# Gates and branch projections with tokens in rows in a hybrid attention / SSD / expert layer

## What is computed

```python
g_na, g_ssd = jnp.split(jax.nn.sigmoid(gates), 2, axis=-1)
mixed = (g_na * (na @ lp['w_na_proj']) + g_ssd * (ssd @ lp['w_ssd_proj'])) @ lp['w_out']
x = x + g1 * mixed
```

## Time and profile before

| | |
|---|---|
| Median of 3 runs | 3015.32 us (3013.15 to 3019.16) |
| Span of the profiled execution | 3014.4 us |
| TensorE busy, in matmuls | 2316.1 us, 77% |
| VectorE busy | 2148.8 us, 71% |
| ScalarE busy | 1338.9 us, 44% |
| GpSimd busy | 1199.5 us, 40% |
| Moved by DMA | 868.48 MB, mean 288 GB/s |

### The profile page before, as it was taken

One profiled execution on the slowest core, in us unless ns is written; L12 is line 12 of the kernel. 1 busy time (PEld: TensorE's weight loads), 2 busy tenths in 40 slices (PEclk: granted clock), 3 DMA queues, 4 the chain that ended last, 5 costly groups with the idle time before them and its releaser, 6 DMA issues.

```text
span 3014.4 us, 39129 instructions
## 1 busy us (share of the span) xinstructions
PE 2316.1 (77%) x15054; PEld 2048.9 (68%) x15054; DVE 2148.8 (71%) x2801; ACT 1338.9 (44%) x2319; POOL 1199.5 (40%) x793
## 2 busy tenths in 40 slices
PE   6799999999999999999999950000233339999997
PEld 2578889988888898999997950000232328888886
DVE  1344445877778853444454699999999988999987
ACT  1233334566777773433334420000698934434443
POOL 0000000134334310000000676666788856767763
PEclk8799999999999999999999985555555559999998
DMA  9887776545454559876554369999999968999996
GB/s 392 329 304 295 291 291 232 184 156 173 172 180 154 173 197 371 319 260 240 191 192 167 140 263 422 392 364 363 403 421 422 422 259 308 372 365 376 361 375 235
DMA packets 152796, 868.48 MB, mean 288 GB/s; under 512 B 18865, under 2 KB 31169, under 8 KB 74705
## 3 DMA queue, kind: packets, MB, share of 16 engines
q1 hardware_dynamic: 68578, 449.03, 40.3%
q0 software_dynamic: 73872, 406.08, 34.8%
q10 hardware_dynamic: 10160, 10.88, 1.0%
HBM read 836.81 MB, written 27.39 MB: 287 GB/s over the span
## 4 chain that ended last, share of the span: by engine, by line
PE 50%; DVE 22%; DMA 9%; POOL 8%; issue 8%; ACT 3%; DVEq 0%; ACTq 0%; SPq 0%; POOLq 0%
PE bank L1805 28%; DVE u_ring L1664 9%; POOL u_ring L730 8%; PE bank L1791 8%; PE bank L2205 7%; DMA raw<-in_tiles 3%; DMA v_got<-in_v_rest,expert 3%; PE bank L1830 2%; DVE w_lo L1210 2%; DVE peer_g L1705 2%; DMA u_ring<-in_peer_u,expert 1%; DVE conv L1324 1%; DMA v_raw<-in_v_dense 1%; PE bank L2180 1%; DVE decay_s L1361 1%
## 5 line engine op out<-in xcount | busy, mean ns | idle before, releaser
L1210 DVE TENSOR_TENSOR w_lo<-raw,w_hi 128x1024 fp32r<-128x1024 f32 x450 | 581.6, 1304 | 564.6 <-ACT w_hi L775 558.6
L775 ACT ACTIVATE w_hi<-raw 128x1024 fp32r<-128x1024 f32 x482 | 500.6, 1057 | 561.1 <-PE bank L1805 327.3
L1805 PE MATMUL bank<-h_lo,w_hi 128*128 128x256 f32 x2048 | 593.7, 290 | 24.7 <-DVE w_lo L1210 16.0
L1805 PE MATMUL bank<-h_hi,w_lo 128*128 128x256 f32 x2048 | 582.8, 285 | 0.0
L1805 PE MATMUL bank<-h_hi,w_hi 128*128 128x256 f32 x2048 | 582.6, 284 | 0.0
L730 POOL DMA_INDIRECT u_ring<-in_peer_u,expert x256 | 508.3, 1985 | 166.7 <-DVE act_p L1664 85.1
L1805 PEld LDWEIGHTS bank<-h_lo,w_hi 128*128 128x128 f32 x2048 | 395.3, 193 | 69.5 <-issue 37.0
L1664 DVE CUSTOM_DVE_ANT_0 u_ring<-u_ring,h_t 128x2048 f32<-128x2048 f32 x192 | 430.7, 2289 | 9.3 <-DMA u_ring<-in_peer_u,expert 7.8
L737 POOL DMA_INDIRECT v_got<-in_v_rest,expert x256 | 358.5, 1401 | 180.1 <-DVE peer_g L1705 137.1
L1805 PEld LDWEIGHTS bank<-h_hi,w_lo 128*128 128x128 f32 x2048 | 395.5, 193 | 0.7
L1805 PEld LDWEIGHTS bank<-h_hi,w_hi 128*128 128x128 f32 x2048 | 395.3, 193 | 0.0
(11 more groups left out here) (317 smaller groups left out, 4760.8 us busy)
## 6 DMA issues: line engine op xcount, KB each, us to landing
raw<-in_tiles SPq DMA_DIRECT2D x337, 1024.0 KB, 5.6
v_raw<-in_v_dense SPq DMA_DIRECT2D x128, 660.0 KB, 7.2
s_t<-in_states POOLq DMA_DIRECT2D x8, 512.0 KB, 7.3
y_hi_rows<-y_hi_e POOLq DMA_DIRECT2D x16, 256.0 KB, 2.4
y_lo_rows<-y_lo_e POOLq DMA_DIRECT2D x16, 256.0 KB, 6.3
gate_rows<-gate_buf ACTq DMA_DIRECT2D x8, 512.0 KB, 6.7
y_hi<-y_hi_rows POOLq DMA_DIRECT2D x8, 512.0 KB, 8.3
y_lo<-y_lo_rows POOLq DMA_DIRECT2D x8, 512.0 KB, 4.2
```

What stands on the lines that cost most here:

```text
L775: act.activation(w_hi[:, i % RING], raw[:, slot % SLOTS, (n % 2) * 2 * CH:(n % 2 + 1) * 2 * CH], ACT.Copy) \
L1210: dve.tensor_tensor(w_lo[:, i % RING], raw[:, n // 2 % SLOTS, (n % 2) * 2 * CH:(n % 2 + 1) * 2 * CH], w_hi[:, i % RING].bitcast(F32), ALU. ...
L1805: ins = pe.matmul(spot if x.shape[1] == KT else spot.rearrange("p (s t) -> p s t", s=NS), w[:, col], moving, start=start and k == 0 and m ...
```

## The change

`gates`, `nap` and `ssd` are made by `tokens_out` in place of `features_out`, so their banks hold tokens in partitions; the gate rows, the products and the sum (`mix_t`, formerly `mix_f`) take that form too, with the same sizes. `tokens_out` gets the arguments that the two depths of `ssd` need. The sum is turned by TensorE: `turn_mix(p)` is eight transposes of 128x128 into banks 4 and 5 or 6 and 7, in the order behind half 1 of `ssd` 2, 4 and 6 and of `out` 0. `mixed_hi` and `mixed_lo` then split it from those banks, behind half 3 of the same. Two pairs of semaphores become one each (`kv_saved` for `k_saved` and `v_saved`, `res_in` for `x2_in` and `g1_in`).

The diff, cut (left out: new shapes in declarations, the renamed semaphores' other uses):

```diff
...
         y_lo = at("y_lo", [P, NS, 2 * KT, P], F32R, 152)
-        gate_n = at("gate_n", [P, 2, 4, T], F32, 48)
-        gate_y = at("gate_y", [P, 2, 4, T], F32, 104)
-        gated = at("gated", [P, 4, T], F32, 184)
-        mix_f = at("mix_f", [P, KT, T], F32, 64)
+        gate_n = at("gate_n", [P, 2, NS, CH], F32, 48)
+        gate_y = at("gate_y", [P, 2, NS, CH], F32, 104)
+        gated = at("gated", [P, NS, CH], F32, 184)
+        mix_t = at("mix_t", [P, 4, NS, CH], F32, 64)
...
         mix_sum = sem("mix_sum")
+        mix_turn = sem("mix_turn")
...
         mix_ready = sem("mix_ready")
-        x2_in = sem("x2_in")
-        g1_in = sem("g1_in")
+        res_in = sem("res_in")
...
-            pool.wait_ge(v_saved, 16)
+            pool.wait_ge(kv_saved, 16 * 5)
...
             for s, name in enumerate(("x_prompt", "x_sample")):
-                pool.dma_start(x2_t[:, s, :], a[name][0]).then_inc(x2_in, 16)
+                pool.dma_start(x2_t[:, s, :], a[name][0]).then_inc(res_in, 16)
...
                 pool.wait_ge(row_saved[n], 64 * len([i for i in saved_rows if i % 2 == n]))
-            pool.dma_start(g_rows[0:8, :], mod_rows[:, 2 * D:3 * D]).then_inc(g1_in, 16)
-            pool.dma_start(g_rows[8:9, :], a["ada_b"][:, 2 * D:3 * D]).then_inc(g1_in, 16)
+            pool.dma_start(g_rows[0:8, :], mod_rows[:, 2 * D:3 * D]).then_inc(res_in, 16)
+            pool.dma_start(g_rows[8:9, :], a["ada_b"][:, 2 * D:3 * D]).then_inc(res_in, 16)
...
                                       row[32 * t:32 * t + NS, i % 2, :]).then_inc(row_saved[i % 2], 16)
+
+            def mixed_hi(p):
+                act.wait_ge(mix_turn, p + 1)
+                for n_ in range(2):
+                    ins = act.activation(mix_hi[:, 4 * p + 2 * n_:4 * p + 2 * n_ + 2, :],
+                                         psum[4 + 2 * (p % 2) + n_][:].rearrange("p (b t) -> p b t", b=2), ACT.Copy)
+                ins.then_inc(mix_split, 1)
...
                     act.wait_ge(evac_a, ACT_DUE[ACC_OF["gates", j]])
-                    act.dma_start(gate_rows[j].rearrange("p b t -> p (b t)"),
+                    act.dma_start(gate_rows[j].rearrange("p s n -> p (s n)"),
                                   gate_buf[:, j % 2].rearrange("p s n -> p (s n)")).then_inc(gate_saved[j % 2], 16)
-                elif kind == "ssd" and j % 2 and h == 7:
-                    p = j // 2
-                    act.wait_ge(mix_sum, p + 1)
-                    act.activation(mix_hi[:, 4 * p:4 * p + 4], mix_f[:, 4 * p:4 * p + 4], ACT.Copy).then_inc(mix_split, 1)
+                elif kind == "ssd" and j and j % 2 == 0 and h == 3:
+                    mixed_hi(j // 2 - 1)
                 elif kind == "out":
+                    if j == 0 and h == 3:
+                        mixed_hi(3)
...
+            def mixed_lo(p):
+                dve.wait_ge(mix_split, p + 1)
+                for n_ in range(2):
+                    b = 4 * p + 2 * n_
+                    ins = dve.tensor_tensor(mix_lo[:, b:b + 2, :],
+                                            psum[4 + 2 * (p % 2) + n_][:].rearrange("p (b t) -> p b t", b=2),
+                                            mix_hi[:, b:b + 2, :].bitcast(F32), ALU.subtract)
+                ins.then_inc(mix_ready, 1)
+
...
                     dve.wait_ge(gate_in[j % 2], 16 * (j // 2) + 16)
-                    for b in range(2):
-                        ins = dve.tensor_tensor(mix_f[:, 4 * j + 2 * b:4 * j + 2 * b + 2, :],
-                                                bank[b][:].rearrange("p (b t) -> p b t", b=2),
-                                                gate_n[:, j % 2, 2 * b:2 * b + 2], ALU.mult)
+                    for s in range(NS):
+                        ins = dve.tensor_tensor(mix_t[:, j, s], bank[s][:], gate_n[:, j % 2, s], ALU.mult)
...
                             dve.wait_ge(row_saved[n_], 64 * len([i for i in saved_rows if i % 2 == n_]))
-                    for b in range(2):
-                        ins = dve.tensor_tensor(gated[:, 2 * b:2 * b + 2], bank[b][:].rearrange("p (b t) -> p b t", b=2),
-                                                gate_y[:, p % 2, 2 * b:2 * b + 2], ALU.mult)
+                    for s in range(NS):
+                        ins = dve.tensor_tensor(gated[:, s], bank[s][:], gate_y[:, p % 2, s], ALU.mult)
...
                     dve.wait_ge(evac_v, DVE_DUE[ACC_OF[kind, j]])
-                    m = mix_f[:, 4 * p:4 * p + 4]
-                    dve.tensor_tensor(m, m, gated[:], ALU.add).then_inc(mix_sum, 1)
-                    dve.wait_ge(mix_sum, p + 1)
-                    dve.wait_ge(mix_split, p + 1)
-                    dve.tensor_tensor(mix_lo[:, 4 * p:4 * p + 4], m, mix_hi[:, 4 * p:4 * p + 4].bitcast(F32),
-                                      ALU.subtract).then_inc(mix_ready, 1)
+                    dve.tensor_tensor(mix_t[:, p], mix_t[:, p], gated[:], ALU.add).then_inc(mix_sum, 1)
+                elif kind == "ssd" and j and j % 2 == 0 and h == 3:
+                    mixed_lo(j // 2 - 1)
+                elif kind == "out" and j == 0 and h == 3:
+                    mixed_lo(3)
...
-            def tokens_out(n, bank, x_hi, x_lo, width=CH):
+            def tokens_out(n, bank, x_hi, x_lo, width=CH, k0=0, start=True, stop=True):
...
                         for m, (x, w) in enumerate(((x_lo, hi), (x_hi, lo), (x_hi, hi))):
-                            ins = pe.matmul(bank[s][:, 0:width], x[:, k, t], w[:, col], start=k == 0 and m == 0,
-                                            stop=k == last and m == 2)
+                            still = x[:, k, t] if x.shape[1] == KT else x[:, s, k0 + k, :]
+                            ins = pe.matmul(bank[s][:, 0:width], still, w[:, col], start=start and k == 0 and m == 0,
+                                            stop=stop and k == last and m == 2)
...
-            def features_out(n, bank, x_hi, x_lo, k0=0, start=True, stop=True):
+            def features_out(n, bank, x_hi, x_lo):
...
                         col = slice(kk * CH + b * P, kk * CH + (b + 1) * P)
-                        spot = bank[b // 2][:, (b % 2) * T:(b % 2 + 1) * T]
                         for m, (w, x) in enumerate(((hi, x_lo), (lo, x_hi), (hi, x_hi))):
-                            moving = x[:, k0 + k, :] if x.shape[1] == KT else x[:, :, k0 + k, :]
-                            ins = pe.matmul(spot if x.shape[1] == KT else spot.rearrange("p (s t) -> p s t", s=NS),
-                                            w[:, col], moving, start=start and k == 0 and m == 0 and b % 2 == 0,
-                                            stop=stop and k == KT - 1 and m == 2, skip_group_check=True)
+                            ins = pe.matmul(bank[b // 2][:, (b % 2) * T:(b % 2 + 1) * T], w[:, col], x[:, k, :],
+                                            start=k == 0 and m == 0 and b % 2 == 0, stop=k == KT - 1 and m == 2,
+                                            skip_group_check=True)
                 ins.then_inc(split_used, 1)
+
+            def turn_mix(p):
+                pe.wait_ge(mix_sum, p + 1)
+                if p >= 2:
+                    pe.wait_ge(mix_ready, p - 1)
+                for s in range(NS):
+                    for b in range(4):
+                        ins = pe.transpose(psum[4 + 2 * (p % 2) + b // 2][:, (b % 2) * T + s * P:(b % 2) * T + (s + 1) * P],
+                                           mix_t[:, p, s, b * P:(b + 1) * P], ident[:])
+                ins.then_inc(mix_turn, 1)
...
                 bank = acc[ACC_OF[kind, j] % 2]
-                if kind in ("q", "k", "bc", "xs", "gates", "wq"):
+                if kind in ("q", "k", "bc", "xs", "wq"):
                     features_out(n, bank, h_hi, h_lo)
-                elif kind in ("v", "z"):
+                elif kind in ("v", "z", "gates"):
...
                 elif kind == "nap":
-                    features_out(n, bank, na_hi, na_lo)
+                    tokens_out(n, bank, na_hi, na_lo)
                 elif kind == "ssd":
-                    features_out(n, bank, y_hi, y_lo, k0=KT * (j % 2), start=j % 2 == 0, stop=j % 2 == 1)
+                    tokens_out(n, bank, y_hi, y_lo, k0=KT * (j % 2), start=j % 2 == 0, stop=j % 2 == 1)
...
                     turn_result(GROUPS - 1, 1)
+                elif kind == "ssd" and j and j % 2 == 0 and h == 1:
+                    turn_mix(j // 2 - 1)
...
                     if h == 1:
+                        if j == 0:
+                            turn_mix(3)
+                            pe.wait_ge(mix_ready, 3)
...
```

More of the change, by code:

```diff
@@ L353, in program @@
         mod_rows = nc.dram_tensor("mod_rows", (8, 6 * D), F32, kind="Internal").ap()
-        gate_rows = nc.dram_tensor("gate_rows", (8, P, 4, T), F32, kind="Internal").ap()
+        gate_rows = nc.dram_tensor("gate_rows", (8, P, NS, CH), F32, kind="Internal").ap()
         na_hi_rows = nc.dram_tensor("na_hi_rows", (P, KT, T), F32R, kind="Internal").ap()
@@ L386, in program @@
```

(18 more changed lines are left out.)

## The result

The changed kernel takes 3001.29 us (median of five runs) against 3016.49 us for the kernel before. One disturbed run of 10968 us counts in that median and not in the ratio, which is 0.9949 (95% interval 0.9934 to 0.9964): 10.9 to 19.9 us less, where 15.8 were forecast. Five more runs of it gave 0.9956 (0.9943 to 0.9969). The profiled execution has a span of 2992.9 us and took 2994.9, so a time lies 2.0 us above its span here; the prediction had taken 0.9.

What follows compares the result with a forecast made beforehand. TensorE alone was taken to bound the steady stretch, with ScalarE beside it in gates 0 and 1 and transfers near their end in gates 2 to 5. -15.0 - 3.0 - 1.5 + 3.8 = -15.7 us, 2999.5 us; range 2994 to 3007.

Steps and rivals of the forecast that it cites:

- steady stretch: Gates 6 and 7 and both projections, 1231.3 to 1554.2: TensorE alone sets the end; 112 halves save 15.0 us.
- behind 1710 only the start counts: After 1710 VectorE is busy 1213.6 of 1304.4 us, so what TensorE saves ahead should pass through whole.
- The main term: 512-column matmuls at 229.1 ns replace pairs of 256 at 120.1: 0.134 us saved a half, 15.0 us in the steady stretch.
- The rule named there: N/2.4 + 2.5 ns a matmul: estimated 5 us saved in 160 halves, 1.2 us after the turns, so no change.
- The turns: Four `turn_mix` of eight fp32 transposes on TensorE's path: 3.8 us added, bounds 3.5 and 7.3 us.
- Rival (c): The turns wait for the sum, VectorE being late: say 7 us a turn, 3027 us; chance 0.04.
- the missing cover: Sum done 2.6 us after the half's end, turn reached at 5.5: 2.9 us of cover; without it each turn stalls.
- Gates 0 and 1: 16 halves beside the last scan group, partly moving up with the scan's products: 1.5 us saved, bounds 0 and 2.1.
- Gates 2 to 5: 16 pairs in 1115 to 1231.3, transfers at 0.96 perhaps refusing some: 3.0 of 4.3 us saved, bounds 0 and 4.3.
- I give the clock no term: Clock granted at 1.00 (2.4 GHz) in all three stretches and TensorE not pausing in the new order: no term.
- rule on HBM: About 358 GB/s a core: gates 2 to 5 already at the limit, term 0 instead of 3.0 us.
- rival (b): Saving partly given back after 1710, where gathers, table transfers and VectorE mesh: half lost, 3007 us; chance 0.12.

Runs made afterwards that it cites:

- both halves of the change: Gates alone by tokens_out on the kernel before, ratio 0.9993; both projections alone, gates again by features_out on the changed kernel, ratio 0.9960.
- version with 256 columns: Changed kernel with each 512-column matmul of gates and both projections cut in two of 256, same operands held; ratio to the kernel before 1.0016.
- late sigmoid: Changed kernel with the sigmoid of gates 1 moved on ScalarE behind half 4 of gates 2; ratio 0.9942.
- both edits: Changed kernel with `na` reloads moved to gates 6, `y_hi` reloads into branch A and the gates 1 sigmoid behind half 4 of gates 2; ratios 0.9923, 0.9930.
- late reloads: Changed kernel with the reloads of `na` moved to gates 6 and those of `y_hi` beside `y_lo` in branch A; ratio 0.9942.
- projections alone: Changed kernel with the gates made by features_out again, so only both projections by tokens_out, plus the turns; ratio 0.9960.
- version with early turns: Changed kernel with each turn ahead of half 0 of the next entry, not behind half 1; gates 6 to the long run 332.3 us for 316.1.

## Why the prediction was right

**What bounds.** TensorE alone in the steady stretch, ScalarE beside it in gates 0 and 1, transfers near their end in gates 2 to 5: these three held. That behind 1710 only the start counts is not contradicted, but the late stretch varies by 10 us, so it is not shown. That both halves of the change add up (14.3 against 14.2) shows that nothing of it was coupled in the steady stretch.

**The main term** had the right mechanism and was mis-sized. The step is the reading of 229.1 ns from 96 matmuls; it took the edge of a run for a part of each matmul. It measured 227.2 and 226.9. The 114 halves ahead of the long run took 328.4 us before (1561.55 - 1.91 - 1231.29) and 310.7 in the changed kernel (the runs of L1802 above, without the turns): 17.7 us saved and not 15.0. The version with 256 columns shows the part of a matmul that does not grow with its columns: 2 x 120.0 - 226.9 = 13.1 ns for the prediction's 11.1.
The rule named there (the Trainium skill, TensorE: Matmul & The Clock Gate, "Back-to-back issue gap") is given by the page for a single matmul. By it the change would have been worthless, an estimate; the trace has 226.9 ns where it gives 215.8, and 120.0 where it gives 109.2, in a stream with a weight load for each matmul.

**The turns** were 3.8 us by forecast, and 3.5 by three readings (the chain, the version without them, the version with 256 columns against the kernel before). They wait for nothing. Rival (c) was no danger as placed, but would have cost 4.1 us a turn and not the missing cover.

**Gates 0 and 1** gave 0.6 of 1.5 us. The step that failed is that the part of the chain with the scan's products "moves up with them". The part with TensorE in it is short. Before, and then in the changed kernel:

```profile
1065.63 5.80 PE bank L1805 x48
...
1073.59 2.88 PE bank L1805 x24
...
1076.91 5.75 PE bank L1805 x48
1082.67 1.85 PE bank L1920 x8
```

```profile
1065.12 5.56 PE bank L1802 x24
...
1072.83 2.77 PE bank L1802 x12
...
1076.15 5.49 PE bank L1802 x24
1081.63 1.83 PE bank L1939 x8
```

Five of the 16 halves lie on this chain, and they give 0.6 us. Behind them it is on ScalarE and VectorE alone until TensorE goes on with its weights (1124.72 before, 1123.65 in the changed kernel), and takes 40.2 us in both. TensorE itself came 2.1 us earlier to the wait (its last work ahead of it ends 55.6 us after the start of gates 0, before 57.7), and stood idle for it: the wait ahead of the second slot grew from 1.36 to 2.92 us. That ScalarE's sigmoid with its table load, ahead of the weight split, was what it waited for is shown by the late sigmoid, which took 2.9 us out.

**Gates 2 to 5** gave 2.7 for 3.0 us, but as two terms, of which the prediction had one. "TensorE does not pause in the new order either, so I give the clock no term" is wrong. After the 2.92 us of idle the clock fell. The stretches of the changed kernel there, and then the same place before, where the idle was 1.36 us:

```profile
1120.70:1123.60 2.90, 0.04 (x4) 0.00 (x0) 1.23 (x2) 2.42 (x5) 0.00 (x0) 1.00 0.61 110
1123.60:1127.00 3.40, 3.35 (x8) 2.67 (x9) 2.84 (x5) 2.60 (x5) 0.00 (x0) 0.50 1.01 422
```

```profile
1122.30:1124.70 2.40, 1.05 (x9) 0.11 (x8) 1.26 (x2) 2.35 (x4) 0.00 (x0) 1.00 0.71 246
1124.70:1128.00 3.30, 3.28 (x27) 3.28 (x28) 2.73 (x4) 2.58 (x5) 0.00 (x0) 1.00 0.90 350
```

The first slot after it took 7.29 us where the later ones take 5.66, 1.6 us lost. Six profiles have an idle of 2.9 us or more at this place (the longest wait listed for TensorE is 2.9 to 3.4); in five the slot took 7.17 to 7.36 us, in one (late reloads) 5.78. The three with 1.4 us (before, projections alone, 256 columns) took 6.01 or 6.02, their full clock's time. Without that the stretch would have given 4.3 us, the whole of its term: a pair to the next takes 6.64 us for 6.91, and 15 of the 16 pairs lie behind the mark.

```profile
1214.16 5.66 PE bank L1802 x24
...
1220.80 5.66 PE bank L1802 x24
```

The transfers did not refuse it. They do refuse more, as the late sigmoid showed. That the fall cost 1.6 us and that both edits remove it is shown; why an idle of 2.9 us makes the clock fall on some occasions and not on others is open.
Of the rule on HBM (the Trainium skill, DMA: Bandwidth & Descriptors, "Where 436 GB/s comes from") that would have set this term to 0: the stretch moved 367 GB/s over 116 us, again more than its 358, with one core at work.

**The sum.** -0.6 - 2.7 - 14.2 = -17.5 us for the forecast's -15.7. Four errors, +2.7 on the halves of the steady stretch, +0.3 on the turns, -0.9 and -0.3 on the gates, partly cancel, and that is luck. The medians of the first five runs and of the second are 15.2 and 14.6 us under those of the kernel before. Between that and 17.5 lies the late stretch, rival (b), or chance; with 10 us from one execution to the next in this stretch the runs do not part them.

## What to carry to other kernels

Take the price of a matmul from a run that is far longer than its edges, and count matmuls: at the full clock a split product of 512 columns costs 227 ns, and two of 256 cost 240 whichever operand is held. Before TensorE is made faster, read which engine hands it its next weights: if that one does not move, the time saved becomes idle time, and an idle time of 2 to 3 us may cost 1.5 to 3 us more in clock. Two waits that take turns to be last are to be removed together; here, in one profile each, one alone gave 0.6 us, the other lost 3.3, and both gave 5.8, then 5.2.

## What was not expected of the hardware

An idle TensorE of 1.7 to 3.4 us was followed by some 3 us, once 6 us, at the lower level (0.50 granted, 1.2 GHz) in part of the cases: after 2.9 us or more at the hand-over to gates 2 in five of six profiles, after two of four waits of 2.8 us in the version with early turns, after waits of 3.4 and 1.9 us with the late sigmoid alone, after 1.7 us at the start of gates 0 in three of twelve, after 1.4 us at the hand-over in none of three. Matmuls of 512 columns start 0.43 us apart then, and one such fall costs 1.4 to 1.7 us, the one of 6 us 3.0. Eight fp32 transposes of 128x128 take 0.87 us in a stream, 109 ns each, about half a matmul of 512 columns.
